# Retention in pieces between the gate tiles, the forget-gate attention behind it, and the first scores ahead of the last gate

## The reference

```python
def even_layer(x, norm_g, w_in, b_f, gn_g, w_out):
    h = rms_norm(x, norm_g)
    u = h @ w_in
    q_f, k_f, v_f, f_l, q_r, k_r, v_r, z = jnp.split(u, EVEN_SPLITS, axis=-1)
    o_f = fox_attention(q_f, k_f, v_f, f_l + b_f)        # 8 heads of 64, causal softmax with a forget gate
    o_r = retention(q_r, k_r, v_r) * gn_g                # 8 heads of 64, causal, decayed, no softmax, group norm
    y = jnp.concatenate([o_f, o_r], axis=-1) * jax.nn.silu(z)
    return x + y @ w_out

def odd_layer(...):
    ...                                                  # 16 heads in 4 groups
    o = nsa_attention(q, kc, vc, ks, vs, kw, vw, gl, ...)
    return x + (o * jax.nn.silu(z)) @ w_out
```

## Time and profile before

| | |
|---|---|
| median of three runs | 1566.89 us (1564.44 to 1569.54) |
| profiled execution | 1566.48 us |
| its span in the trace | 1564.7 us |
| TensorE busy | 1476.0 us (94%) |
| VectorE busy | 973.4 us (62%) |
| ScalarE busy | 882.0 us (56%) |
| TensorE's share of the chain that ended last | 59% |

### The profile page before, as it was taken

One profiled execution on the slowest core, in us unless ns is written; L12 is line 12 of the kernel. 1 busy time (PEld: TensorE's weight loads), 2 busy tenths in 40 slices (PEclk: granted clock), 3 DMA queues, 4 the chain that ended last, 5 costly groups with the idle time before them and its releaser, 6 DMA issues.

```text
span 1564.7 us, 24980 instructions
## 1 busy us (share of the span) xinstructions
PE 1476.0 (94%) x10148; PEld 947.0 (61%) x10148; DVE 973.4 (62%) x1946; ACT 882.0 (56%) x1247; POOL 67.6 (4%) x148
## 2 busy tenths in 40 slices
PE   6999998999989999999998999989699999899997
PEld 3444485665458448585787666445385755466676
DVE  6732547888478566555667224576756336699974
ACT  4544456777554665454553453657354557678862
POOL 0000000000100100000010000001000000000000
PEclk8999999999999999999999999999899999999999
DMA  6233232111422334433325366411023332200002
GB/s 183 87 102 108 87 103 81 55 55 54 156 86 82 129 108 122 119 112 108 108 87 76 97 91 96 94 54 32 21 88 105 117 108 81 81 1 2 2 12 85
DMA packets 127218, 132.07 MB, mean 84 GB/s; under 512 B 9760, under 2 KB 124192, under 8 KB 126976
## 3 DMA queue, kind: packets, MB, share of 16 engines
q1 hardware_dynamic: 124336, 119.59, 27.0%
q0 software_dynamic: 2768, 10.89, 2.0%
HBM read 128.38 MB, written 2.10 MB: 83 GB/s over the span
## 4 chain that ended last, share of the span: by engine, by line
PE 59%; DVE 8%; ACT 4%; issue 2%; DMA 2%; POOL 0%; ACTq 0%; DVEq 0%
PE bank L709 8%; PE bank L710 8%; PE bank L711 8%; PE bank L748 6%; PE bank L750 5%; PE bank L749 5%; PE bank L942 3%; PE bank L924 3%; PE bank L915 2%; DVE wring L1872 2%; PE bank L911 1%; ACT whigh L1274 1%; DMA wring<-in_even_w_in 1%; PE bank L824 1%; DVE scr L2399 1%
## 5 line engine op out<-in xcount | busy, mean ns | idle before, releaser
L709 PE MATMUL bank<-xT,whigh 128*128 128x512 f16 x960 | 366.1, 381 | 10.4 <-DVE xT L2045 7.7
L710 PE MATMUL bank<-xT,whigh 128*128 128x512 f16 x960 | 366.0, 381 | 0.0
L711 PE MATMUL bank<-xT,wring 128*128 128x512 f16 x960 | 365.6, 381 | 0.0
L1872 DVE SCALAR_TENSOR_TENSOR wring<-wring,wsc,whigh 128x2048 f16<-128x2048 f32 x105 | 245.0, 2334 | 165.6 <-ACT whigh L1274 165.1
L1274 ACT ACTIVATE whigh<-wring,wsc 128x2048 f16<-128x2048 f32 x105 | 208.8, 1988 | 156.4 <-DVE wsc L1775 138.0
L1291 ACT ACTIVATE whigh<-wring 128x2048 bf16<-128x2048 f32 x105 | 199.0, 1895 | 121.3 <-DMA wring<-in_even_w_in 43.5
L748 PE MATMUL bank<-whigh,slab 128*128 128x256 f16 x800 | 218.0, 273 | 3.0 <-DVE wring L1872 1.2
L750 PE MATMUL bank<-whigh,slab 128*128 128x256 f16 x800 | 218.1, 273 | 0.0
L749 PE MATMUL bank<-wring,slab 128*128 128x256 f16 x800 | 218.0, 273 | 0.0
L709 PEld LDWEIGHTS bank<-xT,whigh 128*128 128x128 f16 x960 | 94.4, 98 | 126.3 <-DVE xT L2045 7.9
L711 PEld LDWEIGHTS bank<-xT,wring 128*128 128x128 f16 x960 | 94.4, 98 | 114.7 <-issue 2.5
(11 more groups left out here) (324 smaller groups left out, 2356.3 us busy)
## 6 DMA issues: line engine op xcount, KB each, us to landing
wring<-in_w_in SPq DMA_DIRECT2D x28, 1024.0 KB, 5.1
wring<-in_w_up SPq DMA_DIRECT2D x16, 1024.0 KB, 5.3
wring<-in_w_down SPq DMA_DIRECT2D x16, 1024.0 KB, 5.2
wring<-in_even_w_in SPq DMA_DIRECT2D x14, 1024.0 KB, 9.5
wring<-in_odd_w_in SPq DMA_DIRECT2D x14, 1024.0 KB, 4.9
wring<-in_w_a SPq DMA_DIRECT2D x4, 1024.0 KB, 5.2
wring<-in_w_out SPq DMA_DIRECT2D x4, 1024.0 KB, 5.2
wring<-in_even_w_out SPq DMA_DIRECT2D x4, 1024.0 KB, 4.7
```

The costliest lines, as they stand in the source:

```text
L709: pe.matmul(bank, wh[:, k, wcol:wcol + width], xh[:, k, :], start=k == 0, stop=False)
L710: pe.matmul(bank, wh[:, k, wcol:wcol + width], xl[:, k, :], start=False, stop=False)
L711: mm = pe.matmul(bank, wl[:, k, wcol:wcol + width], xh[:, k, :], start=False, stop=k == KC - 1)
L1872: dve.scalar_tensor_tensor(low_of(i)[:, :, 0:m], loaded(i)[:, :, 0:m], wsc[:, n:n + 1], high_of(i)[:, :, 0:m], ALU.mult, ALU.subtract).the ...
```

## The change

- The order of the weight slots of `ze` is turned: features 4 to 7 (the retention's gates) first, then 0 to 3.
- TensorE no longer makes `ze`, then the attention, then the retention. `gates_and_retention` goes through 16 half tiles of `ze` (12 matmuls each), k = 0 to 15, and puts a piece of the retention ahead of each. With m, phase = k / 3 and its rest: phase 0 has the mean of pair m - 1 and two groups of scores of pair m, phase 1 the third group and the variance of pair m - 1, phase 2 the values of pair m. ScalarE and VectorE have their parts of both works in the same rhythm, one step behind, in one list each. The scores use four banks, the retention's output and statistics one each, the gates two in turn.
- The steps 0 and 1 of the forget-gate attention (`EARLY`) stand ahead of the half tiles 14 and 15, the rest behind the gates. For the odd layer the steps 0 and 1 stand ahead of its last gate tile.
- The merged rows are split and multiplied in the order 4, 0, 5, 6, 1, 7, 2, 3; `oe` starts when seven are there and waits for one (row 3). The last variance is no longer inside `oe`.
- `gated_scale` moves from step 2 to step 6, and `norm_bound("rms_o")` from the end of the retention to a place behind the second slot of `oe`, ahead of the low part of its fourth slot.
- The retention's rows and its masked scores lie in other tiles (`slab[2]`, `slab[3]`), the sigmoids in `scr` 4 and 5.

```diff
+        for i, c in enumerate((2, 3, 0, 1)):
+            stream.append(("ze", cols(W, 3080 + SLOTW * c), SLOTW, 2 * i + 2))
...
+        OUT_ROWS = {"o1": tuple(range(8)), "oe": (4, 0, 5, 6, 1, 7, 2, 3), "oo": tuple(range(8))}
...
+            def merged(self):
+
+                own = {VALUE_LAG + len(TILES) * self.branches * (m + 1) + 1: (m, self.name + "_y", m + 1) for m in range(self.heads // 2)}
+                if self.name == "fox":
+                    own.update({i: (row, "yr", 4) for i, row in zip((7, 9, 10, 12), range(4, 8))})
+                assert tuple(own[i][0] for i in sorted(own)) == OUT_ROWS[{"fox": "oe", "nsa": "oo"}[self.name]]
+                return {i: (n, *own[i]) for n, i in enumerate(sorted(own))}
...
                         mm.then_inc(s_(n + "_sc"), 1)
+                    if i == TURN_LAG:
+                        if n == "fox":
+                            pe.wait_ge(s_("rt_rs"), 4)
+                        else:
+                            pe.wait_ge(s_("zo_ev"), n_("zo_ev", 8))
+                    if i == VALUE_LAG:
+                        if n == "fox":
+                            pe.wait_ge(s_("ze_ev"), n_("ze_ev", 8))
+                        else:
+                            pe.wait_ge(s_("ct_ev"), 16)
...
+            def gates_and_retention():
+
+                xh, xl = xhalves
+                for k in range(16):
+                    n, half = divmod(k, 2)
+                    m, phase = divmod(k, 3)
+                    if phase == 0:
+                        if 1 <= m <= 4:
+                            ret_mean(m - 1)
+                        if m < 4:
+                            ret_group(m, 0)
+                            ret_group(m, 1)
+                    if phase == 1:
+                        if m < 4:
+                            ret_group(m, 2)
+                        if 1 <= m <= 4:
+                            ret_variance(m - 1)
+                    if phase == 2 and m < 4:
+                        ret_values(m)
+                    if k == 14:
+                        pe.wait_ge(s_("rt_ea"), 12)
+                        pe.wait_ge(s_("frow_both"), 1)
+                        pe.wait_ge(s_("decay_in"), 32)
+                    if k >= 14:
+                        attention(FOX, EARLY[k - 14:k - 13])
+                    if k == 0:
+                        pe.wait_ge(s_("vr_ev"), n_("vr_ev", 8))
+                    if half == 0:
+                        if n % 2 == 0:
+                            wh, wl = slot("ze")
+                        if n >= 2:
+                            pe.wait_ge(s_("ze_ev"), n_("ze_ev", n - 1))
+                    gate_bank, ww = GATE_BANKS[n % 2], slice(n % 2 * P, n % 2 * P + P)
+                    for c in range(4 * half, 4 * half + 4):
+                        pe.matmul(gate_bank, wh[:, c, ww], xh[:, c, :], start=c == 0, stop=False)
+                        pe.matmul(gate_bank, wh[:, c, ww], xl[:, c, :], start=False, stop=False)
+                        mm = pe.matmul(gate_bank, wl[:, c, ww], xh[:, c, :], start=False, stop=c == KC - 1)
+                    if half == 1:
+                        mm.then_inc(s_("ze_mm"), 1)
...
+            gates_and_retention()
+            attention(FOX, FOX.later)
+            pe.wait_ge(*out_made("oe", 7))
+            tok_and_norm("oe", ohalves["oe"], SA, "rms_o", normed, SB, 1, "kc", SA, out_made("oe", 8))
...
+            def nsa_start():
+                between_gates(7)
+                pe.wait_ge(s_("zo_ev"), n_("zo_ev", 6))
...
+                attention(NSA, EARLY)
+
+            feat("zo", 8, xhalves, ZBANKS, before={7: nsa_start, **{m: lambda m=m: between_gates(m) for m in range(1, 7)}})
...
+            attention(NSA, NSA.later)
...
+                act.wait_ge(s_("ze_mm"), n_("ze_mm", n + 1))
+                if n >= 2:
+                    act.wait_ge(s_("ze_ev"), n_("ze_ev", n - 1))
+                act.activation(scr[:, 4 + n % 2, :], GATE_BANKS[n % 2][:, :], ACT.Sigmoid, scale=undo("ze", n // 2)).then_inc(s_("ze_sg"), 1)
...
+            for k in range(17):
+                m, phase = divmod(k, 3)
+                if phase == 0:
+                    if m < 4:
+                        ret_copy(m, 0)
+                        ret_copy(m, 1)
+                    if 1 <= m <= 4:
+                        pair_square(m - 1)
+                if phase == 1:
+                    if m < 4:
+                        ret_copy(m, 2)
+                    if 1 <= m <= 4:
+                        pair_root(m - 1)
+                if phase == 2 and m < 4:
+                    pair_out_copy(m)
+                if k % 2 == 0 and k >= 2:
+                    gate_sigmoid(k // 2 - 1)
+                if k % 4 == 0 and k < 16:
+                    period("ze", k // 4)
+                if k % 4 == 1:
+                    following("ze", k // 4)
+                if k == 14:
+                    attention(FOX, EARLY)
+            act.wait_ge(s_("ze_ev"), n_("ze_ev", 8))
+            attention(FOX, FOX.later)
+
             out_slots("oe")
             norms(None, "rms_o", SB, "kc", x="oe_x")
...
+                    attention(NSA, EARLY)
+            attention(NSA, NSA.later)
             out_slots("oo")
...
+                    norm_bound(rms)
                 low(slot_at(name, 3))
                 if ln:
...
+                for i in some:
+                    if i == 6:
                         gated_scale(name)
...
+            for k in range(17):
+                m, phase = divmod(k, 3)
+                if phase == 0:
+                    if 1 <= m <= 4:
+                        ret_centre(m - 1)
+                    if m < 4:
+                        ret_mask(m, 0)
+                        ret_mask(m, 1)
+                if phase == 1 and m < 4:
+                    ret_mask(m, 2)
+                if k % 2 == 0 and k >= 2:
+                    even_gate(k // 2 - 1)
+                    even_bound(k // 2 - 1)
+                if phase == 2 and 1 <= m <= 4:
+                    ret_finish(m - 1)
+                if k % 4 == 0 and k < 16:
+                    before("ze", k // 4)
+                if k % 4 == 3:
+                    after("ze", k // 4)
+                if k == 14:
+                    attention(FOX, EARLY)
+            dve.tensor_reduce(xmax[:, 0:1], hmax[:, 0, :], AX_X, ALU.max).then_inc(s_("out_max"), 1)
+
+            attention(FOX, FOX.later)
             add_and_norm("oe", SA, 1.0, None, "rms_o", normed, SB, "kc")
...
+                    attention(NSA, EARLY)
```

283 lines of the change are left out of this document (119 added, 164 removed).

## The result

The changed kernel takes 1571.03 us, median of 20 runs (1567.11 to 1575.17), the kernel before in the same session 1567.01 us (20 runs, 1563.90 to 1569.54). The ratio is 1.0029, 95% interval 1.0021 to 1.0036: 4.5 us slower, where the forecast was 1565.5 us, about 1 us faster. The profiled spans are 1569.3 and 1564.7 us, 4.6 us apart, so the two traces differ by as much as the ratio says.

A forecast was written before the change was run, and what follows sets the result against it. TensorE, busy 94% of the span, was taken as the bound. Even stretch -5.3, norm's bound +2.3, clock +1.7, odd attention's start +0.3 gave -1.0 us from 1566.5, so 1565.5 us; range 1556 to 1573, the forecast's own 1560 to 1570.

The forecast's parts named there:

- the term of the clock: Even attention's start: half-speed rows behind the longer waits at steps 2 and 4, 1.7 us more once, bounds 0 and 10.
- gates and retention: Even layer: TensorE waits of 3.9, 2.8, 5.9 and 5.4 us; attention step 4 starts 39.9 us later.
- The prediction's own sign: Wrong if the granted clock is near 0.5 for more than 5 us between gates and `oe`.
- the clock falls behind every wait: Rival: four waits of 3 to 6 us each leave 5 us at half speed, 2.5 us lost each; 1573.8 us, chance 0.13.
- The odd attention's start: Odd layer: step 4 starts at 1375.3 to 1375.6, 0.3 us more; bounds 7.8 less and 4 more.
- The attention's rest and the first output slot: Even layer from attention step 4: 34.1 us plus 0.5 (0 to 3), then `oe`'s first slot in 10.8 without a gap.
- The norm's bound: VectorE ahead of the low part of `oe`'s fourth slot: nothing covers it, 2.3 us more.
- The table loads: Rival on ScalarE: each load costs its time twice, 9.0 us more, 1574.5 us; chance 0.03.
- Covered after all: Rival, even layer: waits at the variances vanish, only earlier ones remain at the attention's start; 14.5 us go, 1551; chance 0.25.

The follow-up runs named there:

- the kernel with all waits filled: Changed kernel with matmuls added in four even waits and in front of the odd attention's step 4: ratio 1.0001 to the kernel before.
- the kernel with later sizes: Changed kernel with ScalarE's sizes of the even gate's weight slots one piece later: ratio 0.9983 to the kernel before.
- the kernel with the late end of pair 3: Changed kernel with VectorE's end of retention pair 3 moved to step 6 of the even attention: ratio 1.0053, median 1576.81 us.
- the mended kernel: Changed kernel with later sizes, norm's bound earlier, both attentions' early exponentials behind the last sigmoid, even minima before pair 3's end: 1548.78 us, ratio 0.9877.

## Why the prediction was wrong

The forecast was -1.0 us, the measurement +4.5 (3.3 to 5.6). The step that failed is the term of the clock: "I take 1.7 us once, bounds 0 and 10". It measured 4.4 us (2.6 to 6.2), and it was missing where it counts, behind the odd attention's step 4. A second term, gates and retention, was short by a load. Point by point:

- **The clock** (predicted 1.7). Half-speed rows stand behind five waits of 2.84 to 6.05 us, not one. With TensorE kept at work in the even and odd waits 4.4 us go by the ratio; in the odd layer alone 3.9 by the odd stretch, 1.1 in executions where it is short. The mean granted clock says the same over many executions: 0.9789 in the 20 of the changed kernel, 0.9813 in 33 of the kernel before. As an estimate from these, 0.0024 of 1568 us is 3.8 us more of TensorE's clock lost than before, and in the kernel with all waits filled it is 0.9851. The 1.7 us were also worked out from unlike rows: 5.9 us of the odd layer (bf16 bias rows, x4 at the earlier trace rows) against 4.3 of the even one (f32, x8 at the earlier trace rows). The same odd rows at full speed took 3.1 us (1370.66 to 1373.80 with 18 matmuls added to the kernel before), so they lost 2.8. The prediction's own sign came true as well, a clock near 0.5 for more than 5 us between gates and `oe`: it was 0.50 from 1074 to 1080. The rival "the clock falls behind every wait" had the mechanism and a chance of 0.13. Its size, 2.5 us for each, was too high, since part of the slow rows lies beside other waits: the 2.4 us lost at 1075 (steps 2 and 3 and a turn in 6.7 us, 4.3 at full speed in the kernel with later sizes) are followed by a wait of 2.98, the 3.2 us at 1375 by none. The argument used against it (the even steps 2 and 3 of before at full speed behind 3.49 us) was the luck of one trace. In the kernel before with the odd early steps alone, whose even layer is untouched, the same wait has half-speed rows behind it, and the clock was 0.50 from 1038 to 1044:

```profile
1039.15 1.65 PE L911 MATMUL bank<-side 64*128 64x256 f32 x8 [3.49 <-ACT scr L1599]
```

- **The odd attention's start** (predicted +0.3; bounds -7.8 and +4). Step 4's start was right to 0.1 us: 1375.54. The term ended there, and the loss begins there: 3.2 us more from step 4 to step 5. The prediction priced the clock at the even layer only, although the slow stretch of before that it quoted was the odd one's. Measured for the whole part: -4.1 us when undone, +2.7 when made alone.
- **Gates and retention** (predicted step 4 39.9 us later; 42.1, counted from the first gate matmul, and 40.5 to 43.9 in the four other traces with this code). The waits for squares and exponentials were forecast within 0.2 to 2.4 us (pair 3's variance 0.98 for 2.8). Missing was a load: ScalarE's size of the third slot waited 7.66 us for a transfer of 14.0 (984.96 to 999.01; 8.2 in the kernel before at that place), in front of the copy that pair 0's mean needs. The list had the size with 2.1 us and no landing time. Its undoing brings 7.2 us, more than wait and slow rows in their place, since the waits further on shrink too.
- **The attention's rest and the first output slot** (predicted 0.5 more, no gap): 35.1 us from step 4 to its end where 34.1 was, no gap, right within half a microsecond.
- **The norm's bound** (predicted 2.3): the wait is 2.58 for 0.31 before, undone it goes. Right; the run's 3.8 us includes it with its interval of 2.1 either way.
- **The table loads** as a rival: a sigmoid starts 0.02 us behind its load (1366.87 behind 1365.57 plus 1.28), so the extra drain of the Trainium skill ("ScalarE: Activation LUTs", What ACT_TABLE_LOAD costs) is not there in this trace either. What loads cost is their own 1.28 us, where they stand in a chain.
- **Covered after all** (0.25): no; the variances wait.

In sum: the even part was forecast at -1.3 us with its clock term, and is +0.5 (-1.1 to +2.2) by the run with the odd early steps undone, +1.8 by the run with them alone; the odd part was forecast at +0.3, and is +4.1 by the one and +2.7 by the other. Of the miss of 5.5 us the odd attention's start is between 45% and 70%, and most of that its half-speed rows; the rest is the even layer's.

The Trainium skill has the rule ("TensorE: Matmul & The Clock Gate", The HAM clock gate): the clock is released by activity and falls to half when the engine idles. The runs with added matmuls agree (granted clock 1.00 for 0.51 behind the odd wait); the prediction had the effect in one term and not in the others.

Open stays what decides how soon the clock falls and comes back behind one and the same wait, how much of filling all waits is lost against the sum of its parts (4.4 against 8.6 us, the intervals overlap in part) beyond the 2.8 us named above, and what the long executions of the kernel with the late end of pair 3 look like inside.

## What to carry to other kernels

A wait on TensorE has two prices, its length and the half-speed rows behind it; the second counts in full only where TensorE is the bound behind the wait, so ask of every wait that a change moves what runs behind it. Merging two waits of 2 and 4 us into one of 6 can cost more than both. Whether the rows behind a wait ran slowly in one trace is a draw: read several executions before a wait of 3 to 6 us is priced at its length alone. Work pulled ahead on one engine must be pulled ahead on the others in an order of its own: keep the exponentials behind the last sigmoid, and the minima in front of a long pass. A pass that waits for a load belongs behind the short operation that somebody waits for.

## What was not expected of the hardware

A 128x128 fp32 matmul of identity by identity took 0.23 us (25 in 5.75 us at a granted clock of 1.00; the trace has two records for each), while eight fp32 transposes of that size take 1.09 us, 0.14 each. Filler work on TensorE costs nothing itself where it ends before the wait does, and the clock was 1.00 behind waits of 4 to 6 us that it filled. The same wait doesn't cost the same each time: behind the 3.66 us for pair 2's square, which stands in eleven traces at 3.66 or 3.67, the two matmuls took between 1.12 and 2.08 us, and behind the 6.05 us of the odd layer step 4 to step 5 took 6.99 or about 5.2. Executions of the same code spread by 5.6 and 8.1 us here, longer where the mean granted clock was lower (0.976 to 0.981 for the changed kernel), and those of the mended kernel by 2.6 us in four runs.

The clock also fell where TensorE had no gap at all. In the changed kernel, between two gate tiles of the odd layer:

```profile
1322.57 2.50 PE L1101 MATMUL bank<-slab 64*128 64x31 f32 x32
1325.00 1.06 PE L1114 MATMUL bank<-ident,slab 128*31 128x128 f32 x8
1325.89 0.56 PE L735 MATMUL bank<-xT,whigh 128*128 128x512 f16 x1
1326.25 0.63 PE L736 MATMUL bank<-xT,whigh 128*128 128x512 f16 x1
```

The clock is 0.58 over 1326 to 1330, and the gate's matmuls last 0.63 us where they last 0.38 at full speed. Ahead of it stand matmuls of 31 columns and transposes, in which the profile counts TensorE as busy throughout. So a busy TensorE in the profile is no proof of the full clock. No run here varies this.
